# The two expert results of a token combined on TensorE, and the last scaling split over three engines

## What is computed

```python
act = jax.nn.silu(hg) * hu * gates[..., None].astype(h.dtype)     # gates hold w0 and w1, else 0
moe_out = jnp.einsum('tef,efd->td', act, w_down)                  # = w0 * y0 + w1 * y1
x = x + gate2 * moe_out.reshape(x.shape)
...
y = xf * lax.rsqrt(jnp.mean(xf * xf, axis=-1, keepdims=True) + EPS)
return (y * w.astype(jnp.float32)).astype(x.dtype)                # final norm, w = final_norm_w
```

## Time and profile before

| | |
|---|---|
| time, median of 3 runs | 616.38 us (616.27 to 617.57) |
| time of the profiled execution | 621.26 us |
| its span in the trace | 619.4 us |
| PE busy | 492.6 us, 80% of the span |
| DVE busy | 224.1 us, 36% |
| ACT busy | 142.8 us, 23% |
| POOL busy | 86.1 us, 14% |
| last expert matmul ends, start of the tail | 588.56 us into the span |

### The profile page before, as it was taken

One profiled execution on the slowest core, in us unless ns is written; L12 is line 12 of the kernel. 1 busy time (PEld: TensorE's weight loads), 2 busy tenths in 40 slices (PEclk: granted clock), 3 DMA queues, 4 the chain that ended last, 5 costly groups with the idle time before them and its releaser, 6 DMA issues.

```text
span 619.4 us, 7520 instructions
## 1 busy us (share of the span) xinstructions
PE 492.6 (80%) x2624; PEld 234.0 (38%) x2625; DVE 224.1 (36%) x616; ACT 142.8 (23%) x263; POOL 86.1 (14%) x177
## 2 busy tenths in 40 slices
PE   1769889999989999950479899999988878788800
PEld 1225688544478544630243233333332222222200
DVE  3589855999982105560020010110110010101027
ACT  3555842601148201300030010110110010100023
POOL 2000603888000151013000000000000000000030
PEclk9998989999989999975589999999998797978965
DMA  8980340733994931049648993879999999996162
GB/s 296 366 329 0 120 136 6 286 136 120 388 387 183 378 147 43 26 159 392 263 168 335 391 379 108 353 301 411 431 424 423 423 423 422 423 423 266 35 215 107
DMA packets 38032, 164.52 MB, mean 266 GB/s; under 512 B 2776, under 2 KB 3544, under 8 KB 32240
## 3 DMA queue, kind: packets, MB, share of 16 engines
q1 hardware_dynamic: 31120, 145.79, 59.9%
q10 hardware_dynamic: 4608, 10.86, 4.8%
q0 software_dynamic: 2272, 7.46, 3.4%
HBM read 152.76 MB, written 11.34 MB: 265 GB/s over the span
## 4 chain that ended last, share of the span: by engine, by line
issue 51%; PE 30%; DVE 7%; DMA 5%; ACT 4%; POOL 1%; ACTq 0%; POOLq 0%; DVEq 0%
PE psum L604 7%; PE psum L487 3%; PE psum L553 3%; PE psum L479 3%; DMA arena<-in_x_sample 3%; PE psum L509 3%; PE psum L578 3%; PE psum L418 2%; DMA arena<-in_w_mod 2%; PE psum L598 2%; PE psum L628 1%; ACT arena L802 1%; POOL sorted_tokens L1519 1%; DMA arena<-sorted_outputs,pos_u 1%; PE psum L496 1%
## 5 line engine op out<-in xcount | busy, mean ns | idle before, releaser
L676 PE MATMUL psum<-arena 128*64 128x512 f32 x672 | 165.2, 648 | 31.5 <-DMA arena<-in_w_up 21.2
L676 PEld LDWEIGHTS psum<-arena 128*64 128x64 f32 x672 | 51.9, 148 | 131.2 <-issue 111.6
L689 PE MATMUL psum<-arena 128*64 128x512 f32 x336 | 75.8, 592 | 2.3 <-ACTq L972 2.3
L1364 DVE TENSOR_TENSOR arena<-arena,psum 128x256 f32<-128x256 f32 x21 | 8.9, 422 | 183.4 <-ACT arena L956 183.4
L1527 POOL DMA_INDIRECT arena<-sorted_outputs,pos_u x6 | 5.7, 952 | 308.6 <-DMA sorted_outputs<-arena 307.1
L689 PEld LDWEIGHTS psum<-arena 128*64 128x64 f32 x336 | 25.1, 137 | 48.8 <-issue 48.8
L956 ACT ACTIVATE arena<-psum 128x256 f32<-128x256 f32 x21 | 8.1, 384 | 146.2 <-PE psum L676 130.7
L604 PE MATMUL psum<-arena 128*128 128x512 f32 x96 | 41.5, 592 | 0.0
L418 PE MATMUL psum<-arena 128*2 128x256 f32 x256 | 30.7, 395 | 0.3 <-DMA arena<-in_w_mod 0.3
L660 PE MATMUL psum<-arena 128*128 128x128 f32 x48 | 6.7, 302 | 27.0 <-DMA arena<-sorted_tokens 27.0
L961 ACT ACTIVATE arena<-psum 128x512 f32<-128x512 f32 x21 | 12.5, 597 | 66.7 <-PE psum L689 66.7
(11 more groups left out here) (278 smaller groups left out, 586.2 us busy)
## 6 DMA issues: line engine op xcount, KB each, us to landing
arena<-in_w_gate SPq DMA_DIRECT2D x16, 2048.0 KB, 17.5
arena<-in_w_up SPq DMA_DIRECT2D x16, 2048.0 KB, 22.3
arena<-in_w_down SPq DMA_DIRECT2D x16, 2048.0 KB, 19.8
arena<-in_w_mod SPq DMA_DIRECT2D x12, 2048.0 KB, 13.8
arena<-in_w_in SPq DMA_DIRECT2D x3, 2048.0 KB, 19.1
sorted_outputs<-arena ACTq DMA_DIRECT2D x42, 128.0 KB, 6.5
arena<-in_w_out SPq DMA_DIRECT2D x2, 2048.0 KB, 17.5
arena<-modulation_rows ACTq DMA_DIRECT2D x3, 1024.0 KB, 11.2
```

What stands on the lines that cost most here:

```text
L676: last = mm(bank[0][HALF * t:HALF * t + HALF, :], xs[:, k, :], gu[:, :, k, t * 256:t * 256 + 256], start=(k == 0), stop=(k == KD - 1))
L689: last = mm(bank[4][HALF * h:HALF * h + HALF, :], hiddenT[:, s * P + t * HALF:s * P + t * HALF + HALF], dn[:, 2 * t + s, h * 512:h * 512 + ...
```

## The change

The two results of a token are weighted and added by TensorE. For each tile and each `k` there is a 128 x 128 matrix `weigh` that has the tile's weights on its diagonal and zeros elsewhere; `weigh^T @ picked` scales each row by its weight, and the products for k = 0 and k = 1 add up in PSUM. GpSimd builds the six matrices from `ident` during the experts. VectorE then reads the sum from PSUM. The final scaling of tiles 0 and 1 is split in two instructions: ScalarE multiplies by `rstd`, GpSimd by `fnw`. Tile 2 keeps the single instruction on VectorE, and has a semaphore of its own, `final_done_v`.

```diff
+        weigh = view(slot(2), 2 * NT, P)
...
             for t in range(NT):
-                sp.wait_ge(S("final_done"), t + 1)
+                sp.wait_ge(S("final_done") if t < 2 else S("final_done_v"), t + 1 if t < 2 else 1)
                 dst = io["out_p"][0] if t == 0 else io["out_s"][0, (t - 1) * P:t * P, :]
                 sp.dma_start(dst, X[:, t, :]).then_inc(S("out_done"), 16)
...
+            pe.wait_ge(S("weigh_made"), 1)
+            pe.wait_ge(S("combine_free"), 1)
+            for t in range(NT):
+                pe.wait_ge(S(f"picked_in{t}"), 32)
+                for h in range(2):
+                    for k in range(2):
+                        last = mm(bank[(0, 2, 6)[t] + h][:, :], weigh[:, 3 * k + t, :],
+                                  picked[:, t, k, h * 512:h * 512 + 512], start=(k == 0), stop=(k == 1))
+                last.then_inc(S("combined"), 1)
...
-            def first_choice(t):
-                act.wait_ge(S(f"picked_in{t}"), 32)
-                A(picked[:, t, 0, :], picked[:, t, 0, :], ACT.Copy, scale=wts[:, t:t + 1]).then_inc(S("y0_done"), 1)
-
-            first_choice(0)
+            act.sem_inc(S("combine_free"), 1)
+            act.wait_ge(S("fnw_in"), 16)
+
+            def scale_rows(t):
+                act.wait_ge(S("rstd3_done"), t + 1)
+                A(X[:, t, :], X[:, t, :], ACT.Copy, scale=st[:, 6 + t:7 + t]).then_inc(S("scaled"), 1)
+
             for t in range(NT):
-                if t + 1 < NT:
-                    first_choice(t + 1)
                 act.wait_ge(S("x2_done"), t + 1)
                 a(A(picked[:, t, 0, :], X[:, t, :], ACT.Square, accum_out=st[:, t:t + 1]))
                 a.settle()
                 A(st[:, 3 + t:4 + t], st[:, t:t + 1], ACT.Sqrt, bias=epsc[:, 0:1],
                   scale=1.0 / D).then_inc(S("root3_done"), 1)
+                if 0 < t:
+                    scale_rows(t - 1)
...
-            def final_norm(t):
+
+            def rstd(t):
                 dve.wait_ge(S("root3_done"), t + 1)
-                v(V_.reciprocal(st[:, 6 + t:7 + t], st[:, 3 + t:4 + t]))
-                stt(X[:, t, :], X[:, t, :], st[:, 6 + t:7 + t], fnw[:, :], ALU.mult,
-                    ALU.mult).then_inc(S("final_done"), 1)
-
+                V_.reciprocal(st[:, 6 + t:7 + t], st[:, 3 + t:4 + t]).then_inc(S("rstd3_done"), 1)
+
+            for t in range(NT):
+                dve.wait_ge(S("combined"), t + 1)
+                b = (0, 2, 6)[t]
+                v(tt(picked[:, t, 1, :], psum[:, b:b + 2, :].rearrange("p a b -> p (a b)"), g2rows[:, min(t, 1), :],
+                     ALU.mult))
+                if t > 0:
+                    rstd(t - 1)
+                tt(X[:, t, :], X[:, t, :], picked[:, t, 1, :], ALU.add).then_inc(S("x2_done"), 1)
+            rstd(NT - 1)
+            dve.wait_ge(S("rstd3_done"), NT)
             dve.wait_ge(S("fnw_in"), 16)
-            for t in range(NT):
-                dve.wait_ge(S("y0_done"), t + 1)
-                y0, y1 = picked[:, t, 0, :], picked[:, t, 1, :]
-                v(stt(y0, y1, wts[:, 3 + t:4 + t], y0, ALU.mult, ALU.add))
-                v(tt(y0, y0, g2rows[:, min(t, 1), :], ALU.mult))
-                tt(X[:, t, :], X[:, t, :], y0, ALU.add).then_inc(S("x2_done"), 1)
-                if t > 0:
-                    final_norm(t - 1)
-            final_norm(NT - 1)
+            stt(X[:, 2, :], X[:, 2, :], st[:, 8:9], fnw[:, :], ALU.mult, ALU.mult).then_inc(S("final_done_v"), 1)
...
+            pool.wait_ge(S("downed"), 14 * PASSES + 1)
+            pool.wait_ge(S("weights_done"), 1)
+            for c in range(2 * NT):
+                last = p(G.tensor_scalar(weigh[:, c, :], ident[:, :], wts[:, c:c + 1], None, ALU.mult))
+            p.settle()
+            pool.sem_inc(S("weigh_made"), 1)
             pool.wait_ge(S("written"), 32 * (NE * PASSES + 1))
...
+            pool.wait_ge(S("fnw_in"), 16)
+            for t in range(NT - 1):
+                pool.wait_ge(S("scaled"), t + 1)
+                G.tensor_tensor(X[:, t, :], X[:, t, :], fnw[:, :], ALU.mult).then_inc(S("final_done"), 1)
```

More of the change, by code:

```diff
@@ L1350, in _ @@
             v(tt(wts[:, 3:6], pair[:, 3:6], st[:, 24:27], ALU.mult))
+            dve.sem_inc(S("weights_done"), 1)
             def sorted_copy(t):
```

## The result

The changed kernel is slower, as forecast, but by more than forecast, and outside the range: 621.42 us (median of 8 runs, 618.86 to 624.36) against 616.33 (8 runs), a ratio of 1.0080 with a 95% interval of 1.0052 to 1.0109, that is +4.9 us (+3.2 to +6.7). The forecast was 617.9, +1.5. Measured twice more beside the experiments, the ratio was 1.0029 (1.0001 to 1.0056) and 1.0069 (1.0041 to 1.0097).

A forecast was written before the change was run, and what follows sets the result against it. VectorE's 15.65 us were taken to bound the tail; 2.5 (later start) - 4.4 (VectorE and ScalarE) + 2.1 (ScalarE, GpSimd at the end) + 1.3 (second transfer) = +1.5 us on 616.38 gave 617.9 us, range 616.3 to 619.1.

The forecast's parts named there:

- What bounds the tail, and where it starts: End of program: VectorE's 15.65 us bound the tail; nothing changes until the first gathers land at 598.99.
- The diagonal products: GpSimd during the experts: six products needing 6 us, from about 557 and due by 592, hidden.
- TensorE, tile 0: First combining: four products 0.86 us apart, ending at 602.75, 3.7 us against ScalarE's 1.15 for weighting.
- Tiles 1 and 2: Later combining on TensorE: ready at 606.2 and 609.6 if the clock stays low; at most 1 us shows.
- The clock: TensorE after idling: granted clock 0.50, 1.2 GHz, from 599 to 603, spacing products 0.86 us apart.
- Rival 2: Low clock through all twelve TensorE products: tile 2 combined at 609.6, everything behind 0.8 later, 618.7 us; chance 0.12.
- rival 3: TensorE products at full clock: VectorE starts at about 601, total 616.3 us, the same as before; chance 0.1.
- The 0.45 before VectorE's first instruction: Start of VectorE's tail work: an unexplained delay, possibly 0 to 0.5 us, taken as 0.45.
- PSUM read, round trip, reciprocals waiting for ScalarE: VectorE's tail: read 1.23 us, about 2.85 per tile round VectorE and ScalarE, tile 0's reciprocal adding a 0.4 wait.
- GpSimd: Tile 1's multiply by `fnw` at the end: some 2.25 us, done at 616.5, the last thing ready.
- rival 1: GpSimd and VectorE hold each other up in the final norms: up to 0.84 us more, 618.7 us; chance 0.13.
- The second transfer: Last two outputs leave together: the second lands 3.9 us after the first issue, adding 1.3 us.

The follow-up runs named there:

- diag_only: The kernel before plus only GpSimd's six diagonal products, which nobody reads; ratio to before 0.9992, tail 31.0 us.
- half_products: The changed kernel with only the k = 0 products, 12 matmul instructions instead of 24; ratio to before 1.0026, tail 33.1 us.
- warm: The changed kernel plus eleven useless TensorE products while it waits for the first gathers; ratio to before 1.0023, tail 33.9 us.
- pool_alone: The changed kernel with VectorE's final norm of tile 2 held back until GpSimd finished both products; tail 35.5 us, one execution.
- norm_dve: The changed kernel with tile 1's final norm given back to VectorE, tile 0 still split; ratio to before 1.0066, tail 34.0 us.
- swap_out: The changed kernel with SyncE's outputs in the order tile 0, 2, 1; ratio to before 1.0038, tail 34.8 us.
- split_only: The kernel before with only the final scaling of tiles 0 and 1 split over ScalarE and GpSimd; ratio to before 1.0045, tail 33.2 us.
- warm_combine: The changed kernel with all final norms on VectorE as before, plus eleven useless TensorE products; ratio to before 0.9946, tail 30.5 us.
- busy_only: The kernel before plus GpSimd's diagonal products and eighteen useless TensorE products after the last expert matmul; ratio to before 1.0021, tail 30.8 us.
- tile2_warm: The kernel before with only tile 2 combined on TensorE, behind eighteen useless TensorE products; ratio to before 0.9951, tail 29.6 us.

## Why the prediction was wrong

- **What bounds the tail, and where it starts: right.** The landing of the first gathers is 10.6 us behind the last expert matmul, 10.45 before; all that changed lies behind it. The diagonal products are covered, as forecast: 3.5 us on GpSimd, from 550.9, and diag_only has the tail of before within 0.2.
- **TensorE, tile 0: wrong, and the main fault.** "Four 128x512 products with 128x128 weights" are eight matmul instructions. The row I quoted for the duration shows it: line 604 has 96 instructions, and its loops (3 tiles, 2 halves, 8 values of `k`) call it 48 times. I took the time of an instruction and the number from the source. The steps of line 676 in the earlier trace rows hid it: there, with weights of 64 columns, two instructions go in each step, 16 steps for an expert's 16 products, so a product costs one step. With 128 columns one instruction goes in a step, as the rows of line 759 show, and a product costs two. The four instructions reckoned, "ends at 602.75", take 3.7 us, and half_products measured 3.75; the eight took 5.84. The Trainium skill gives four passes for a true f32 product in "FP8 and Floating Point Precision", section "TensorE Precision Notes". The rows show two instructions for each product, 0.43 us each at 2.4 GHz; that each makes two of the four passes would fit, but no run here shows it.
- **Tiles 1 and 2: wrong for the same reason.** "at most 1 us of this shows": at full clock each tile takes 3.4 us, more than the 2.9 of one trip round VectorE and ScalarE, so TensorE set the pace and VectorE waited 0.51 and 0.89.
- **The clock: right**, 0.50 at the start and 1.00 from about 600; with eight instructions it weighed 2.2 us. Rival 2, a clock that stays low throughout, did not come, and rival 3, full clock from the start, neither.
- **The 0.45 before VectorE's first instruction: right**, 0.48 in the change, warm and half_products, 0.5 before. Ahead of tiles 1 and 2 VectorE starts within 0.1 us of TensorE's end. The cause stays open; I had carried the number over from the same place.
- **PSUM read, round trip, reciprocals waiting for ScalarE: right**; the read takes 1.22 for the 1.23 taken.
- **GpSimd: the path right, its price 2.86 for 2.25.** Of the 0.6 us, 0.1 is the price alone (2.34) and 0.5 is rival 1, which did happen: GpSimd's product of tile 0 held VectorE's last norm up (1.55 for 1.28), and this norm held GpSimd's product of tile 1 up. pool_alone and norm_dve show it.
- **The second transfer: right**, 3.6 us from its issue to landing where one alone takes 2.6, 4.0 behind the first issue (3.9 forecast), and 1.0 us back in swap_out.

Sum: forecast 1.5; +2.7 for the twelve instructions more, +0.6 for GpSimd's product, 0.1 unassigned: 4.9, the tail. Without the miscount the forecast would have stood 0.8 us too low, and its direction, slower, rests on the parts that were right: split_only alone is slower by 2.3 us of tail.

One thing stays open. warm_combine is 3.3 us faster with a tail only 0.3 shorter; busy_only shows that the extra products alone bring no such gain. Its interval (2.0 to 4.6) leaves out what its tail says, and that of tile2_warm (1.5 to 4.5, tail 1.3 shorter) just does too. In warm_combine's one profile the experts take 284.6 us, as in before's, so its gain isn't in them either; in tile2_warm's they take 2.4 less. All that can be said is that the twelve times of warm_combine lie between 614.3 and 617.8, where the 35 of before beside it lie between 615.4 and 623.0. I have no cause for it.

## What to carry to other kernels

Count instructions in the profile, not in the source: compare the count of a row with the loops that make it before its duration is used for something new. Work given to an idle TensorE costs two instructions for each f32 product here, and starts at the low clock; it shortened the tail only after products of no use had kept the clock up, by 1.3 us for the last tile alone and by 0.3 for all three. Work moved off the bounding engine must end sooner than that engine would have been done: here 1.28 us on VectorE became 1.13 on ScalarE and then 2.86 on GpSimd at the very end, and GpSimd and VectorE stand in each other's way.

## What was not expected of the hardware

- A VectorE instruction with two operands in SBUF that starts during a GpSimd product waits for its end: 3.37 us for 1.28. Started first, it keeps its time (1.21), and GpSimd takes 2.40 to 3.29 for 2.34, by the overlap.
- Two f32 instructions per product on TensorE, 0.43 us each at 2.4 GHz and 0.85 at 1.2 GHz for 512 columns.
